# Half units of 512-column products for the first mixer's first gates, summed by VectorE

## The reference

```python
xn = _rmsnorm(x, mix_norm[l])
h = xn @ w_in[l]
lru_x, lru_gate, q, k, v, qi, ki, wi, gate_a, gate_b = _split_cols(h)
...
ya = _rg_lru(ua, ...)                       # scan over time, gates r and i from block products
ya = (ya * jax.nn.gelu(lru_gate)) @ w_lru_br[l]
yb = _dsa_attention(qh, kh, vh, qih, ki, wih, rel_bias) @ w_attn_br[l]
merged = jax.nn.sigmoid(gate_a) * ya + jax.nn.sigmoid(gate_b) * yb
x = x + merged @ w_out[l]
```

## Time and profile before

| what | value |
|---|---|
| median of 3 executions | 1043.41 us (1043.38 to 1043.68) |
| profiled execution | 1043.4 us, of which the span from first to last instruction is 1041.6 us |
| mean granted clock of TensorE | 1.000 |
| TensorE busy with products | 1033.7 us, 99% of the span |
| VectorE busy | 774.5 us, 74% |
| ScalarE busy | 590.1 us, 57% |
| GpSimd busy | 179.4 us, 17% |
| chain that ended last | TensorE 86%, VectorE 9% |

### The profile page before, as it was taken

How to read it: one execution, slowest core, us unless ns; L and a number is a source line. 1 busy time by engine, 2 the same in 40 slices (tenths; PEclk the granted TensorE clock), 3 DMA queues, 4 the chain that set the end, 5 groups by cost and what they waited for, 6 DMA issues and landing times.

```text
span 1041.6 us, 17753 instructions
## 1 busy us (share of the span) xinstructions
PE 1033.7 (99%) x6776; PEld 941.3 (90%) x6776; DVE 774.5 (74%) x940; ACT 590.1 (57%) x823; POOL 179.4 (17%) x200
## 2 busy tenths in 40 slices
PE   9999999999999999999999999999999999999997
PEld 8999999899888888899888888999989998888886
DVE  5899875758999997558888866575686688788653
ACT  5765799445656555367544544446577455544532
POOL 0300000222312221022322220010000222222200
PEclk9999999999999999999999999999999999999999
DMA  8744376755767667556767665665435557666551
GB/s 248 240 158 142 122 216 197 234 163 163 197 171 195 176 192 208 176 169 184 206 185 200 181 178 168 206 199 162 158 126 163 182 160 204 187 181 196 169 194 41
DMA packets 272801, 187.45 MB, mean 180 GB/s; under 512 B 6535, under 2 KB 263622, under 8 KB 272742
## 3 DMA queue, kind: packets, MB, share of 16 engines
q1 hardware_dynamic: 272478, 186.28, 60.1%
q10 hardware_dynamic: 264, 0.35, 0.1%
HBM read 185.46 MB, written 1.08 MB: 179 GB/s over the span
## 4 chain that ended last, share of the span: by engine, by line
PE 86%; DVE 9%; issue 3%; ACT 2%; DVEq 0%; ACTq 0%; POOL 0%; POOLq 0%
PE psum L2022 19%; PE psum L1986 19%; PE psum L1991 10%; PE psum L2536 6%; DVE wl L1350 5%; PE psum L2539 3%; PE psum L2585 3%; PE psum L1961 2%; PE psum L1962 2%; PE psum L1963 2%; PE psum L2494 2%; PE psum L2492 2%; PE psum L2493 2%; DVE logit L1783 2%; PE psum L2588 1%
## 5 line engine op out<-in xcount | busy, mean ns | idle before, releaser
L1350 DVE TENSOR_TENSOR wl<-raw,wh 128x2048 fp32r<-128x2048 f32 (+3 forms) x198 | 415.3, 2111 | 99.6 <-ACT wh L663 99.2
L663 ACT ACTIVATE wh<-raw 128x2048 fp32r<-128x2048 f32 (+3 forms) x199 | 328.7, 1667 | 43.3 <-PE psum L2494 25.0
L1986 PE MATMUL psum<-parts,wh 128*128 128x512 f32 x1226 | 294.2, 391 | 0.0
L1986 PEld LDWEIGHTS psum<-parts,wh 128*128 128x128 f32 x1226 | 224.8, 188 | 43.9 <-DVE wl L1350 0.5
L2022 PE MATMUL psum<-parts,wh 128*128 128x256 f32 x1120 | 203.4, 285 | 0.0
L2022 PEld LDWEIGHTS psum<-parts,wh 128*128 128x128 f32 x1120 | 173.8, 192 | 1.4 <-issue 1.0
L1991 PEld LDWEIGHTS psum<-parts,wl 128*128 128x128 f32 x1226 | 158.0, 191 | 6.5
L1991 PE MATMUL psum<-parts,wl 128*128 128x256 f32 x1226 | 160.0, 283 | 0.0
L2022 PE MATMUL psum<-parts,wl 128*128 128x256 f32 x560 | 155.8, 283 | 0.0
L1032 ACT ACTIVATE page_q<-psum 128x512 f32<-128x512 f32 x68 | 40.4, 594 | 121.4 <-PE psum L1991 121.2
L2022 PEld LDWEIGHTS psum<-parts,wl 128*128 128x128 f32 x560 | 106.3, 192 | 0.0
(11 more groups left out here) (279 smaller groups left out, 1331.7 us busy)
## 6 DMA issues: line engine op xcount, KB each, us to landing
raw<-in_ffn_w_in SPq DMA_DIRECT2D x88, 512.0 KB
raw<-in_w_up SPq DMA_DIRECT2D x48, 512.0 KB
raw<-in_w_in SPq DMA_DIRECT2D x23, 1024.0 KB
raw<-in_w_mix_in SPq DMA_DIRECT2D x20, 1024.0 KB
raw<-in_w_down SPq DMA_DIRECT2D x24, 512.0 KB
raw<-in_ffn_w_out SPq DMA_DIRECT2D x10, 1024.0 KB
raw<-in_ffn_w_out SPq DMA_DIRECT2D x16, 448.0 KB
raw<-in_ffn_w_out SPq DMA_DIRECT2D x10, 512.0 KB
```

Of the source, the lines that this page charges most:

```text
L663: act.activation(place(wh, u), place(raw, u), ACT.Copy).then_inc(rounded, 1)
L1350: dve.tensor_tensor(place(wl, u), place(raw, u), place(wh, u).bitcast(F32), ALU.subtract).then_inc(rest, 1)
L1986: mm(banks[base + s], wh[:, u % RING, w:w + P], both[:, t0 + k, :, :].rearrange("p h t -> p (h t)"), start=(k == 0), stop=False)
```

## The change

The four GA units are computed in the other form, half by half. Half h (0 to 7) goes into bank h % 3 and fills it with two addends of 256 columns. VectorE adds them, reading the bank and writing `page_q` (eight reductions); ScalarE's tanh then works in place in `page_q` and waits for the sums instead of for TensorE. The eight sums are put into VectorE's queue at given places. As GA now uses eight banks instead of four, the banks of the eight groups after it (RI1 and GB) move on by one, and RI1's first three groups wait for sums 6, 7 and 8.

```diff
-READER = {n: "A" for n in ("V", "Q", "LG0", "LG1", "LG2", "LG3", "RI0", "GA", "RI1", "GB", "PR",
+READER = {n: "A" for n in ("V", "Q", "LG0", "LG1", "LG2", "LG3", "RI0", "RI1", "GB", "PR",
                            "PG", "KA", "VA", "QB", "KB", "VB", "GA'", "GB'")}
+READER["GA"] = "-"
@@ bank
+            if group(U["RI1"]) <= g < group(U["YB"]):
+                return banks[(g + 1) % 3]
             return banks[g % 3]
+        def gate_a_bank(h):
+            return banks[(group(U["GA"]) + h) % 3]
@@ ScalarE
                 round_unit(20 + m)
-                if m == 0:
-                    act.wait_ge(s_done, 12)
                 if m == 3:
                     y_high(0)
-                evac(group(U["GA"] + m), page_q[:, 2 * m:2 * m + 2, :], func=ACT.Tanh, scale=0.5)
+                act.wait_ge(gate_a_added, 2 * m + 2)
+                act.activation(page_q[:, 2 * m:2 * m + 2, :], page_q[:, 2 * m:2 * m + 2, :], ACT.Tanh, scale=0.5)
@@ VectorE
+            def gate_a_sum(m, s):
+                h = 2 * m + s
+                if s == 0:
+                    dve.wait_ge(gate_a_half, m + 1)
+                else:
+                    dve.wait_ge(mm_done, group(U["GA"]) + m + 1)
+                dve.tensor_reduce(page_q[:, h, :], gate_a_bank(h).rearrange("p (a t) -> p t a", a=2), AX, ALU.add).then_inc(gate_a_added, 1)
             lru_input(0)
+            dve.wait_ge(s_done, 12)
+            gate_a_sum(0, 0)
+            gate_a_sum(0, 1)
             rest_unit(20)
             o_low(4)
+            gate_a_sum(1, 0)
             lru_scan(0)
+            gate_a_sum(1, 1)
             rest_unit(21)
+            gate_a_sum(2, 0)
             o_low(5)
+            gate_a_sum(2, 1)
             lru_output(0)
-            for u in range(22, 25):
-                rest_unit(u)
+            rest_unit(22)
+            rest_unit(23)
+            gate_a_sum(3, 0)
+            gate_a_sum(3, 1)
+            rest_unit(24)
@@ TensorE, bank_free
+                elif group(U["RI1"]) <= g < group(U["RI1"]) + 3:
+                    pe.wait_ge(gate_a_added, 6 + g - group(U["RI1"]))
@@ TensorE
-            pair(18)
+            def gate_a_unit(m):
+                u = U["GA"] + m
+                unit_ready(u)
+                for s in range(2):
+                    h = 2 * m + s
+                    if h < 3:
+                        pe.wait_ge(read_a, READ_BY["A"][group(U["GA"]) - 2 + h])
+                    else:
+                        pe.wait_ge(gate_a_added, h - 2)
+                    for k in range(K):
+                        mm(gate_a_bank(h), wh[:, u % RING, k * 256 + s * P:k * 256 + s * P + P], xx[:, k, :, :].rearrange("p h t -> p (h t)"),
+                           start=(k == 0), stop=False)
+                    for k in range(K):
+                        ins = mm(gate_a_bank(h)[:, 0:T], wl[:, u % RING, k * 256 + s * P:k * 256 + s * P + P], xx[:, k, 0, :],
+                                 start=False, stop=(k == K - 1))
+                    ins.then_inc((gate_a_half, mm_done)[s], 1)
+            gate_a_unit(0)
             turn(5)
             values(4)
-            pair(19)
+            gate_a_unit(1)
             values(5)
-            for u in range(20, 22):
-                pair(u)
+            gate_a_unit(2)
+            gate_a_unit(3)
             lru_gates(1)
```

More of the change, by code:

```diff
@@ L381, in build @@
         merged_done = sem("merged_done")
+        gate_a_half, gate_a_added = sem("gate_a_half"), sem("gate_a_added")
         half_done, half_low, half_added = sem("half_done"), sem("half_low"), sem("half_added")
```

## The result

The changed kernel takes 1047.49 us, the median of 8 executions (1046.10 to 1048.01), against 1043.41 (8 executions, 1043.28 to 1043.68): a ratio of 1.0038, 95% interval 1.0029 to 1.0047. The forecast was 1046.4 with a range of 1044.8 to 1049.2. It is 4.1 us slower, and its runs spread over 1.9 us where those of the kernel before spread over 0.4.

What follows compares the result with a forecast made beforehand. TensorE's own work was taken as the bound, with the stretch's end set by VectorE's and ScalarE's chain: 1043.4 + 2.95 = 1046.4 us, the four units' 0.64 saving already inside. Own range 1045.6 to 1047.4; 8-in-10 range 1044.8 to 1049.2.

Steps and rivals of the forecast that it cites:

- The bound: TensorE, busy all 52 of 52 us in the stretch, bounds the kernel; any wait put into its queue is added to the end.
- The half units: On TensorE, the four GA units in the new form take 5.59 us instead of 5.75, saving 0.64 us over four.
- The price of a sum: Each VectorE reduction takes 0.69 us, with ends of 0.42 and 1.22 kept for the range.
- The chain of the queues: VectorE and ScalarE, with five sums one behind another, set the stretch's end; unit 23 starts 2.95 us late.
- sum (1,1): Third sum on VectorE, behind the scans: done at 148.04, making ScalarE's second GA tanh 2.05 us late.
- the last pair: Last two sums, behind unit 23's weights on VectorE: TensorE waits 2.2 us for bank 0 ahead of RI1's second group.
- the term of the clock: Rival: TensorE's clock falls to 1.2 GHz for RI1's groups and unit 23, at most 7.8 us more, 1054.2; chance 0.03.
- dear sums: Rival: VectorE's strided reductions take up to 1.22 us each, giving 1049.0 us; chance 0.15.
- Same: Rival: ScalarE makes up its delay, only the last sums' order counts, unit 23 0.7 us late, 1044.1; chance 0.15.
- The load of a table after its wait: Rival: ScalarE's table load comes after the second tanh's wait, 1.28 us more, 1047.6; chance 0.05.

## Why the prediction came out as it did

**The bound.** That TensorE gives every wait to the end held: the GB units end 4.13 us later, the time is 4.1 us longer.

**The half units** save 0.16 us each, as the trace without sums shows. In the changed kernel the saving is lost ahead of unit 21, as forecast: its weights come late, and a faster TensorE just waits longer for them.

**The price of a sum** was taken as 0.69 us and is 0.68, so the ends of 0.42 and 1.22 fell away. Addends 256 elements apart in PSUM took no longer than the 512 elements side by side of the earlier trace rows (0.686).

**The chain of the queues**, forecast against measured, in us: first tanh 140.01, 139.98; scans end 147.44, 147.47; sum (1,1) done 148.04, 148.05; unit 21 150.28, 150.30; second tanh 148.08, 148.08; unit 23's weights 155.88, 155.80; last tanh 159.42, 159.33; RI1's second group 158.81, 158.75. (The tanhs out of SBUF take 0.61 to 0.63 us instead of 0.60, less than the 0.05 more each that was put in, hence part of the 0.08 at unit 23's weights.) The place of the sums in the queues is shown by moving them. That about five of them lie on the chain fits doubling them (4.2 us against 3.6 to 4.0); that the delay has two sources, by moving each by itself (2.1 us for sum (1,1), 3.2 for the last pair; both together 3.3, as they overlap and GpSimd takes a part).

**Where it fell short** is the term of the clock. The forecast put the case at 0.03, and at up to 7.8 us, from the sentence that TensorE would stand idle 2.2 us; the likeliest case had no fall in it. It did fall, for some 3.4 us rather than for the 7.8 us of work that I let it last. It took about 0.8 us up to unit 23 (162.39 against the 161.6 forecast for a clock that stays) and 0.4 behind it (23.44 against 23.04), 1.2 together. The run with the wait filled gives the same 1.2 us (1047.49 to 1046.30, with 1046.4 forecast for a clock that stays) and the spread goes with it. My error was in the chance. The mechanism was among the rivals and the size of the wait was right, but I took the wait of 1.1 us in the earlier trace rows as one that TensorE's clock had stood. It is no such evidence. It lies ahead of the very first product, and the ten products behind it run at half the pace of the same product later on (TensorE's timeline of the kernel before):

```profile
1.11 4.64 PE L2196 MATMUL psum<-ones 128*128 128x256 f32 x10 [1.11 <-POOL ones L1230]
...
7.19 0.60 PE L2196 MATMUL psum<-ones 128*128 128x256 f32 x2
```

The ten start 0.43 us apart, the two 0.22. So the kernel before had no wait of this kind to learn from, and the chance of 0.03 rested on nothing measured.

**Luck.** 1047.49 lies just outside the forecast's own range, which ended at 1047.4. The wide range holds it only because its upper end, 1049.2, was left open for dear sums, and these did not come: the clock filled that room.

**The rules weighed.** The second tanh did not wait for its table load, over at 146.84, 1.24 us early. The figure of 2.66 us in the Trainium skill, "ScalarE: Activation LUTs", section "What ACT_TABLE_LOAD costs", would have made it 0.1 us late. The tanh starts 0.03 us behind the sum, so the trace shows no such drain; behind ScalarE's next load, at 149.00, the gelus start at 150.30, 1.30 us later. The Trainium skill, "TensorE: Matmul & The Clock Gate", section "The HAM clock gate", says that the clock gate throttles an idle array. The trace agrees, if late: 0.50 is granted at 161 to 163 us, when the array is busy again behind its wait.

**The rivals.** "Same" (0.7 us late, ScalarE making up its delay) was wrong on the point named: ScalarE made nothing up, since its delay of 2.05 us at the second tanh is 2.13 at round_unit(23), and the wait for the last sums makes it 3.25 at round_unit(24). With the bank wait removed 2.2 us of the loss remain. The load of a table after its wait, and dear sums, did not come.

## What to carry to other kernels

When a reader moves from one engine to another, the new instruction's place in each queue can cost more than its duration: eight sums of 0.68 us were paid with idle time that VectorE had, but their places delayed two other engines by 4.1 us. Put a sum where its input is just ready, ahead of long work that waits for something else, and once a bank is freed by another engine, move the old reader (here the tanh) back to where nobody waits behind it. Removing one hold may show the next (the bank, then the weights), so follow all queues to the point where the lateness is gone.

## What the runs showed of the hardware that was not expected

**TensorE's clock fell behind a short wait.** After 2.1 us between two starts (156.61 to 158.75), following a wait of 0.8 us ahead of unit 21, the granted clock went to the 1.2 GHz level for some 3.4 us, at 159.8, a microsecond after the products had started again. It did not fall, in the trace with sum (1,1) moved, behind waits of 1.2 and 0.3 us, nor, in the trace with RI1's banks moved, behind three of 0.6 to 0.8. With the sums doubled it fell again, at 161.7, inside a wait of 3.1 us. In the changed kernel, the time varied by 1.9 us from run to run; where TensorE was kept busy, by 0.55. One run of each was traced, but every run's mean granted clock is on record. The two shortest runs of the changed kernel (1046.10 and 1046.35 us) have 0.999, the other six (1047.13 to 1048.01) 0.997 or 0.998. A fall like the traced one takes 1.7 us of 1045, or 0.0016, off the mean, so the two short runs had no such fall, and they came out at the 1046.4 forecast for a clock that stays. Why the clock stays up in some runs and not in others is open.

**VectorE and GpSimd wait for each other, and the first one wins.** `wl = raw - wh` with both inputs in SBUF takes 2.28 us, one of GpSimd's two subtractions 1.29 (the second one in the changed kernel, at 159.18, and in the kernel before, at 157.09, where VectorE was idle throughout). Where one starts inside the other, the later one ends a fixed time behind the end of the earlier one. VectorE ends 2.15 us behind GpSimd's operation: 158.09 to 160.24 when it had started 0.03 us after GpSimd (3.42 us in all), and 156.63 to 158.78 when it had started 0.64 after it (2.80). GpSimd ends 1.13 to 1.15 us behind VectorE's: 158.09 to 159.22 in the changed kernel, and 164.17 to 165.32 behind L1653 with y_high(0) moved. So nothing is shared: the later one stands still until the earlier one is done, and then takes nearly its whole own time, 0.13 to 0.16 us less than by itself. The Trainium skill, "SBUF — State Buffer", section "SBUF: two separate sides", says that a VectorE operation with two SBUF inputs and a GpSimd operation that reads SBUF contend for a shared pair of ports, that whichever starts first holds it for the whole instruction, and that the other blocks. The trace agrees, with the numbers above. When the two start within 0.03 us of each other, as with the last pair moved, the time of a run comes out in one of two bunches 1.3 us apart; that the lower bunch is the one in which VectorE was first is argued, not traced.
